# Two transformer blocks on one core: the moving operand of the products read in pairs of tokens 1 KB apart

## The reference, cut to what matters

```
x = first_block(...)     # diff attention + latent attention, then a feed-forward
    h    = rmsnorm(x) * (1 + scale) + shift          # shift, scale, gate from silu(c) @ w_ada + b_ada
    proj = h @ w_in                                  # 3904 columns
    mix  = concat(o_diff, o_mla) @ w_out;  x = x + gate * mix
    f    = square(relu(h2 @ w_ff1)) @ w_ff2          # 2048 -> 8192 -> 2048
    x    = x + gate_f * f;  return rmsnorm(x)
x = second_block(...)    # block-sparse and top-k attention, gated, then a feed-forward
    proj = h @ w_in_2
    y = (sigmoid(ga) * (o_a @ w_moba_out) + sigmoid(gb) * (o_b @ w_dsa_out)) @ w_o
    f = square(relu(h2 @ w_ff1_2)) @ w_ff2_2         # 2048 -> 8192 -> 2048
```

## Time and profile before

| | |
|---|---|
| median of 3 runs | 2734.39 us (2734.12 to 2735.15) |
| profiled execution: span, and its own time as the page gives it | 2736.3 us |
| TensorE matmuls busy | 2649.9 us, 97% |
| VectorE busy | 1938.3 us, 71% |
| ScalarE busy | 1112.3 us, 41% |
| DMA | 658.80 MB, mean 241 GB/s |
| chain that ended last | TensorE 85%, VectorE 7%, DMA 4%, ScalarE 2% |

### The profile page before, as it was taken

One profiled execution on the slowest core, in us unless ns is written; L12 is line 12 of the kernel. 1 busy time (PEld: TensorE's weight loads), 2 busy tenths in 40 slices (PEclk: granted clock), 3 DMA queues, 4 the chain that ended last, 5 costly groups with the idle time before them and its releaser, 6 DMA issues.

```text
span 2736.3 us, 54234 instructions
## 1 busy us (share of the span) xinstructions
PE 2649.9 (97%) x21636; PEld 2485.7 (91%) x21636; DVE 1938.3 (71%) x2030; ACT 1112.3 (41%) x1271; POOL 172.1 (6%) x281
## 2 busy tenths in 40 slices
PE   5999999999999999999998999999999999999998
PEld 2776778899999999998998989999979999999997
DVE  2475586877787776878867888888776565574664
ACT  2333443443343433434333444444444334443443
POOL 5000000101010010110000000001010000000000
PEclk8999999999999999999999999999999999999998
DMA  9997856588888887886766765568847676676763
GB/s 363 368 347 267 264 184 206 190 282 298 284 293 287 274 304 233 294 275 202 252 206 197 223 212 174 163 219 281 285 154 234 196 231 214 193 245 199 231 195 112
DMA packets 304452, 658.80 MB, mean 241 GB/s; under 512 B 31200, under 2 KB 37688, under 8 KB 303928
## 3 DMA queue, kind: packets, MB, share of 16 engines
q1 hardware_dynamic: 272056, 539.35, 58.6%
q0 software_dynamic: 32256, 117.45, 13.3%
HBM read 654.62 MB, written 2.10 MB: 240 GB/s over the span
## 4 chain that ended last, share of the span: by engine, by line
PE 85%; DVE 7%; DMA 4%; ACT 2%; issue 1%; SPq 1%; ACTq 0%; DVEq 0%; POOLq 0%
PE ps L1853 25%; PE ps L1855 24%; PE ps L1854 24%; DVE lo L1039 2%; PE ps L1896 2%; DMA proj<-in_w_ada 2%; PE ps L1898 2%; DMA raw<-in_w_in 2%; PE ps L1897 2%; ACT hi L634 1%; PE ps L2047 1%; DMA ada_ring<-in_w_ada 1%; DVE proj L1211 1%; DVE work L1051 1%; PE ps L1839 1%
## 5 line engine op out<-in xcount | busy, mean ns | idle before, releaser
L1039 DVE TENSOR_TENSOR lo<-raw,hi 128x1024 fp32r<-128x1024 f32 x868 | 1049.5, 1222 | 628.8 <-ACT hi L634 626.9
L634 ACT ACTIVATE hi<-raw 128x1024 fp32r<-128x1024 f32 x868 | 910.4, 1059 | 1267.6 <-PE ps L1855 970.4
L1853 PE MATMUL ps<-acts,hi 128*128 128x256 f32 x4432 | 1247.4, 281 | 21.2 <-DVE lo L1039 13.6
L1854 PE MATMUL ps<-acts,hi 128*128 128x256 f32 x4432 | 1234.3, 279 | 0.0
L1855 PE MATMUL ps<-acts,lo 128*128 128x256 f32 x4432 | 1233.9, 278 | 0.0
L1853 PEld LDWEIGHTS ps<-acts,hi 128*128 128x128 f32 x4432 | 838.7, 189 | 57.5 <-issue 29.9
L1854 PEld LDWEIGHTS ps<-acts,hi 128*128 128x128 f32 x4432 | 836.8, 189 | 1.7 <-issue 1.0
L1855 PEld LDWEIGHTS ps<-acts,lo 128*128 128x128 f32 x4432 | 837.4, 189 | 0.4
L1853 PE MATMUL ps<-f_acts,hi 128*128 128x256 f32 x2048 | 567.6, 277 | 1.4 <-DVE lo L1039 1.3
L1854 PE MATMUL ps<-f_acts,hi 128*128 128x256 f32 x2048 | 565.8, 276 | 0.0
L1855 PE MATMUL ps<-f_acts,lo 128*128 128x256 f32 x2048 | 565.8, 276 | 0.0
(11 more groups left out here) (267 smaller groups left out, 1370.5 us busy)
## 6 DMA issues: line engine op xcount, KB each, us to landing
raw<-in_w_ff SPq DMA_DIRECT2D x512, 512.0 KB, 4.7
raw<-in_w_in SPq DMA_DIRECT2D x232, 512.0 KB, 4.6
ada_ring<-in_w_ada POOLq DMA_DIRECT2D x224, 512.0 KB, 5.0
proj<-in_w_ada SPq DMA_DIRECT2D x92, 512.0 KB, 8.6
ada_ring<-in_w_ada SPq DMA_DIRECT2D x40, 512.0 KB, 6.3
raw<-in_w_out SPq DMA_DIRECT2D x32, 512.0 KB, 5.3
raw<-in_w_o SPq DMA_DIRECT2D x32, 512.0 KB, 5.4
work<-in_w_ada SPq DMA_DIRECT2D x28, 512.0 KB, 6.2
```

The lines of the kernel that those rows point to most:

```text
L634: nc.scalar.activation(hi[n % SPLIT][:, :], raw[n % RAW][:, :], ACT.Copy).then_inc(hi_ready, 1)
L1039: V.tensor_tensor(lo[n % SPLIT][:, :], raw[n % RAW][:, :], hi[n % SPLIT][:, :].bitcast(F32), ALU.subtract)\
L1853: M(out, h, right[:, 0:S], start=start, stop=False)
L1854: M(out, h, right[:, S:2 * S], start=False, stop=False)
```

## The change

Two things change together.

1. The columns of one tile of `acts` and `f_acts` are stored as four runs of 128: high parts of tokens 0 to 127, low parts of tokens 0 to 127, high parts of tokens 128 to 255, low parts of tokens 128 to 255. High parts of token n and token n + 128 are then 256 columns, 1 KB, apart.
2. A product's moving operand still has 256 columns, but in the order n = 0 of both halves, n = 1 of both halves, and so on. PSUM therefore holds token n at column 2n and token n + 128 at column 2n + 1. Each eviction reads every other column (`natural`) and writes two runs of 128 (`halves`), so that all tiles outside `acts` and `f_acts` are as before.

```diff
+        halves = lambda x: x.rearrange("p (a n) -> p a n", a=2) if len(x.shape) == 2 else x.rearrange("p k (a n) -> p k a n", a=2)
+        natural = lambda x: x.rearrange("p (n a) -> p a n", a=2) if len(x.shape) == 2 else x.rearrange("p k (n a) -> p k a n", a=2)
+        places = lambda x: [x.rearrange("p k (a w n) -> p w k a n", a=2, w=2)[:, w] for w in range(2)]
+        acts_hi, acts_lo = places(acts[:, :, :])
+        f_hi, f_lo = places(f_acts[:, :, :])
+        moved = lambda x: x.rearrange("p a n -> p n a")
...
             def product(h, l, right, out, start, stop):
 
-                M(out, h, right[:, 0:S], start=start, stop=False)
-                M(out, h, right[:, S:2 * S], start=False, stop=False)
-                return M(out, l, right[:, 0:S], start=False, stop=stop)
+                right_hi, right_lo = moved(right[0]), moved(right[1])
+                M(out, h, right_hi, start=start, stop=False)
+                M(out, h, right_lo, start=False, stop=False)
+                return M(out, l, right_hi, start=False, stop=stop)
...
-                    xh, xl = acts[:, k, t * P:(t + 1) * P], acts[:, k, S + t * P:S + (t + 1) * P]
+                    xh, xl = acts_hi[:, k, t, :], acts_lo[:, k, t, :]
...
             def plain(dst):
                 def run(left):
-                    V.tensor_copy(dst, left).then_inc(group_out, 1)
+                    V.tensor_copy(halves(dst), natural(left)).then_inc(group_out, 1)
...
-                        last = V.scalar_tensor_tensor(xT[:, tile, :], left[:, j, :], mod(gate, tile), xT[:, tile, :], ALU.mult, ALU.add)
+                        last = V.scalar_tensor_tensor(halves(xT[:, tile, :]), natural(left[:, j, :]), mod(gate, tile), halves(xT[:, tile, :]), ALU.mult, ALU.add)
...
-                    V.tensor_scalar(cross[:, :, :], left, 0.0, None, ALU.max).then_inc(relued, 1)
+                    V.tensor_scalar(halves(cross[:, :, :]), natural(left), 0.0, None, ALU.max).then_inc(relued, 1)
                     dve.wait_ge(relued, k + 1 + dk)
-                    V.tensor_tensor(cross[:, :, :], cross[:, :, :], left, ALU.mult).then_inc(squared, 1)
+                    V.tensor_tensor(halves(cross[:, :, :]), halves(cross[:, :, :]), natural(left), ALU.mult).then_inc(squared, 1)
                     dve.wait_ge(ff_hi, k + 1 + dk)
-                    V.tensor_tensor(f_acts[:, tile, S:2 * S], cross[:, :, :], f_acts[:, tile, 0:S].bitcast(F32), ALU.subtract)\
+                    V.tensor_tensor(f_lo[:, tile], halves(cross[:, :, :]), f_hi[:, tile].bitcast(F32), ALU.subtract)\
                         .then_inc(group_out, 1)
...
-                    V.tensor_tensor(y[:, tile, :], y[:, tile, :], left, ALU.add).then_inc(group_out, 1)
+                    V.tensor_tensor(halves(y[:, tile, :]), halves(y[:, tile, :]), natural(left), ALU.add).then_inc(group_out, 1)
...
-                            last = nc.scalar.activation(acts[:, tile0 + t, 0:S], norm_tmp[:, t, :], ACT.Identity,
+                            last = nc.scalar.activation(acts_hi[:, tile0 + t], halves(norm_tmp[:, t, :]), ACT.Identity,
```

More of the change, by code:

```diff
@@ L645, in group @@
                     act.wait_ge(squared, up + 1 + dup)
-                    nc.scalar.activation(f_acts[:, tile, 0:S], cross[:, :, :], ACT.Copy).then_inc(ff_hi, 1)
+                    nc.scalar.activation(f_hi[:, tile], halves(cross[:, :, :]), ACT.Copy).then_inc(ff_hi, 1)
                 if kind == "gate":
@@ L759, in block_hi @@
                     k = 8 * b + t
-                    last = nc.scalar.activation(acts[:, k, 0:S], block_tmp[:, t, :], ACT.Identity, bias=mods[:, k:k + 1])
+                    last = nc.scalar.activation(acts_hi[:, k], halves(block_tmp[:, t, :]), ACT.Identity, bias=mods[:, k:k + 1])
                 last.then_inc(n_hi, 1)
@@ L1133, in run @@
                 def run(left):
-                    V.tensor_tensor(proj[:, tile, :], proj[:, tile, :], left, ALU.mult).then_inc(group_out, 1)
+                    V.tensor_tensor(halves(proj[:, tile, :]), halves(proj[:, tile, :]), natural(left), ALU.mult).then_inc(group_out, 1)
                 return run
@@ L1140, in run @@
                     dve.wait_ge(group_out, first["dsa"][1] + k)
-                    V.tensor_tensor(cross[:, :, :], proj[:, other, :], left, ALU.mult).then_inc(gated, 1)
+                    V.tensor_tensor(halves(cross[:, :, :]), halves(proj[:, other, :]), natural(left), ALU.mult).then_inc(gated, 1)
                     dve.wait_ge(gated, k + 1)
@@ L1204, in low @@
                     for t in range(a, b):
-                        last = V.scalar_tensor_tensor(acts[:, t, S:2 * S], norm_tmp[:, t, :], shift(t),
-                                                      acts[:, t, 0:S].bitcast(F32), ALU.add, ALU.subtract)
+                        last = V.scalar_tensor_tensor(acts_lo[:, t], halves(norm_tmp[:, t, :]), shift(t),
+                                                      acts_hi[:, t].bitcast(F32), ALU.add, ALU.subtract)
                     last.then_inc(acts_ready, 1)
@@ L1312, in block_low @@
                     k = 8 * b + t
-                    last = V.scalar_tensor_tensor(acts[:, k, S:2 * S], block_tmp[:, t, :], mod(0, k),
-                                                  acts[:, k, 0:S].bitcast(F32), ALU.add, ALU.subtract)
+                    last = V.scalar_tensor_tensor(acts_lo[:, k], halves(block_tmp[:, t, :]), mod(0, k),
+                                                  acts_hi[:, k].bitcast(F32), ALU.add, ALU.subtract)
                 last.then_inc(acts_ready, 1)
@@ L1440, in head_low @@
                     dve.wait_ge(dn_hi, h + 1)
-                    last = V.tensor_tensor(acts[:, 4 * h:4 * h + 4, S:2 * S], work[:, 4 + h, :].rearrange("p (j n) -> p j n", n=S),
-                                           acts[:, 4 * h:4 * h + 4, 0:S].bitcast(F32), ALU.subtract)
+                    last = V.tensor_tensor(acts_lo[:, 4 * h:4 * h + 4], halves(work[:, 4 + h, :].rearrange("p (j n) -> p j n", n=S)),
+                                           acts_hi[:, 4 * h:4 * h + 4].bitcast(F32), ALU.subtract)
                 last.then_inc(o_split, 1)
@@ L1876, in group @@
                             js = slice(j * P, min((j + 1) * P, width))
-                            last = product(h[:, t, js], l[:, t, js], src[:, tile0 + k, :], out[0:js.stop - js.start, at, :],
+                            last = product(h[:, t, js], l[:, t, js], (src[0][:, tile0 + k], src[1][:, tile0 + k]), out[0:js.stop - js.start, at, :],
                                            k == 0 and at % 2 == 0, k == CK * per - 1 and (at % 2 == 1 or at + 1 not in places))
@@ L2025, in start_chunk @@
                         js = slice(j * P, (j + 1) * P)
-                        last = product(h[:, t, js], l[:, t, js], acts[:, k, :], ps[:, 2 * g + j // 2, (j % 2) * S:(j % 2 + 1) * S],
+                        last = product(h[:, t, js], l[:, t, js], (acts_hi[:, k], acts_lo[:, k]), ps[:, 2 * g + j // 2, (j % 2) * S:(j % 2 + 1) * S],
                                        k == 0 and j % 2 == 0, k == KT - 1 and j % 2 == 1)
@@ L2197, in _ @@
                     for t in range(2):
-                        product(h[:, t, j, 0, :], l[:, t, j, 0, :], acts[:, 12 + t, :], out[:, j, :], t == 0, t == 1)
+                        product(h[:, t, j, 0, :], l[:, t, j, 0, :], (acts_hi[:, 12 + t], acts_lo[:, 12 + t]), out[:, j, :], t == 0, t == 1)
                 for q in range(QT):
@@ L2291, in _ @@
                         js = slice(j * P, (j + 1) * P)
-                        last = product(h[:, t, js], l[:, t, js], acts[:, k, :], out[:, j, :], p == out1_first[g] and t == 0 and j % 2 == 0,
+                        last = product(h[:, t, js], l[:, t, js], (acts_hi[:, k], acts_lo[:, k]), out[:, j, :], p == out1_first[g] and t == 0 and j % 2 == 0,
                                        p == out1_last[g] and t == CK - 1 and j % 2 == 1)
@@ L2393, in feed_forward @@
                 for q in range(4):
-                    group(n0 + (4 + q) * FULL, g0 + 4 + q, src=f_acts, fresh={KT - 4: (group_out, g0 + 4)} if q == 0 else None, after=after(q))
+                    group(n0 + (4 + q) * FULL, g0 + 4 + q, src=(f_hi, f_lo), fresh={KT - 4: (group_out, g0 + 4)} if q == 0 else None, after=after(q))
             feed_forward("ff1", "ffn", lambda q: {4: lambda: piece_stats("final", q - 1)} if q else {})
```

46 lines of the change are left out of this document (23 added, 23 removed).

## The result

| | before | after |
|---|---|---|
| median | 2734.26 us (2727.11 to 2735.15, 4 runs) | 2698.41 us (2698.25 to 2702.76, 4 runs) |
| ratio | | 0.9876, 95% interval 0.9851 to 0.9900 |
| profiled span | 2736.3 us | 2696.9 us |

The change makes the kernel 36 us faster. The forecast was 2652, which is 82 us: the direction was right, the size less than half of it. The time still lies just inside the forecast's own range, 2628 to 2700.

The account below looks back on a forecast made before the run. TensorE's matmuls, busy 97% of the span, were taken as the bound: 2736.3 - 85 (94.8 gained less 9.5) + 3 (evictions, copies) = 2654, with the median 1.9 lower, 2652 us; own range 2628 to 2700, with rivals (a) and (c) 2628 to 2816.

Parts of the forecast that it names:

- TensorE is the bound and its spacing is the price: Whole kernel: TensorE's matmuls are busy 97% of the span; a product costs its spacing in the stream, 113.2 or 118.0 ns.
- The loss in line order lies in how the moving operand is read: Products of 256 columns: 6.5 ns of 113.2 are lost by how reads fall, which the new order alters.
- half reading rate: Ground for the gain: two places in turn are each read at half rate, where fp32 passes lose only 2 to 3 ns.
- The two levels come from two streams colliding, the weight load among them: Product streams: an interruption shifts two streams against each other, and the spacing stays at 113.2 or 118.0 ns.
- I take 109.0: Spacing in ns of a product after the change, leaving only the issue loss; gain 24.6 + 70.2 = 94.8 us.
- rival (a): Products: the loss sits in the array or with the weight loads, not in reading order; 2737 us, chance 0.14.
- Slow level in 2,728 matmuls: Ten stretches of TensorE, 322.0 us, stand at 118.0 ns; bringing them to 109.0 gains 24.6 us.
- Give-back of a tenth, 9.5 us: Waits for DMA, such as feed-forward weights, take back a tenth of the 94.8 us gain; 85 us remain.
- Evictions 2 us, copies 1 us, value products 0: Costs: stepped PSUM reads 2 us, split writes of high and low parts 1 us, value groups' untouched moving weights 0.
- Rival (b): All products: each column costs its own fetch, at the fp32 passes' two cycles a column; 4725 us, chance 0.18.
- Rival (c): All products: the new order falls into the slower level, 118.0 ns, everywhere; +80 us, 2814 us, chance 0.09.

Follow-up runs that it names:

- e6: The kernel before, in line order, with 32 of 128 weight columns in 14 of 16 feature tiles: 2730.24 us.
- e1: A kernel of only 60-matmul fp32r streams, varying reading order, distance and weights: 256 columns in line 113.5 or 117.8 ns, pairs 111.7 ns.
- e4: A kernel of only matmul streams, varying weight widths, shifts, closer pairs, 512 columns and bf16: pairs 111.7 ns with 128 weight columns, 109.2 with 96.
- e8: A kernel of only matmul streams with other numbers of moving and weight columns: 111.7 ns beside 128 weight columns for 128 to 256 moving columns in pairs.
- e5: The changed kernel, in pairs, with 32 of 128 weight columns in 14 of 16 feature tiles: 2661.91 us.
- e2: The changed kernel with its four runs of 128 kept, but products and evictions reading in line: 2734.02 us, ratio 0.9997 to the kernel before.
- e9: The changed kernel run once more, unaltered, for a comparison on one chip: 2699.84 us, ratio 0.9881 to the kernel before.
- e10: The changed kernel with the value groups' moving weights also read in pairs: 2693.13 us, ratio 0.9861 to the kernel before.

## Why the prediction was off, step by step

- **TensorE is the bound and its spacing is the price: right.** The span followed TensorE's busy time, 39.4 of 45.9 us.
- **The loss in line order lies in how the moving operand is read: right.** e6 and the narrow and equal-column streams of e1 leave it at 113.7, bf16 doesn't have it (109.2), and alternating two places takes it away. The prediction's half reading rate as a ground is not borne out, though: four places in turn read each at a quarter rate, and stand at 142. That the alternation works is shown; why is open.
- **The two levels come from two streams colliding, the weight load among them: not borne out.** The slow level went with the change (three stretches above), as expected, but e4 has both levels beside 16 weight columns, and no other engine is at work in those streams. Weights do bear on line order (64 columns 119.0, shifts 117.3 to 120.0 in e1), but no run ties the levels to them. What sets the level after an interruption stays open.
- **"I take 109.0" for a product with 128 weight columns: the failed step.** The floor of 109.0 was worked out from rows at two cycles a moving column, where a weight load of 128 columns has 213 ns or more to hide in. No row of before had fp32r weights beside a moving operand that could have gone faster than they, and the weight load was costed at nothing. It takes 111.7 ns (e8) and now sets the pace; e5, where it is narrow, has the forecast's pace and most of the missing time. Redone with 111.7, the term is 2,728 x (118.0 - 111.7) = 17.2 and 16,712 x (113.2 - 111.7) = 25.1, 42.3 us where 94.8 stood. The forecast itself named "the weight loads, which are as before" only in rival (a), as the place of the whole loss, and not as a second limit just under the first. The upper end of its own range, 2700, was for a stream that sheds less than the whole loss, without a word on what would stop it; that the time fell inside is luck, as far as the cause goes.
- **Slow level in 2,728 matmuls: a little low.** By the distances of starts some 3,560 gaps were at 117.8; that lifts 42.3 toward the 45.9 measured. In e2, in the same order, it was some 1,990: this share differs from run to run.
- **Give-back of a tenth, 9.5 us: about right in size.** 6.5 us went to TensorE's waits. The rows show where: TensorE's largest wait, before and after (5.7 us more), then ScalarE's after (90.9 before).

```profile
PE ps L1853 <- DVE lo L1039: 14.9, 8, 5.3
...
PE ps L1861 <- DVE lo L1046: 20.6, 13, 4.9
...
ACT hi L641 <- DMA raw<-in_w_ff: 125.9, 63, 3.9
```

  The first 205 us, at a DMA share of 0.95, gave nothing: they hold 1,249 matmuls now (1,258 in e9), 1,258 before.
- **Evictions 2 us, copies 1 us, value products 0:** 0 for all three, by the rows above. "Whichever way the reads go" missed that the value groups had the same loss to shed, 576 x 13 ns (e10).
- **Rival (a), the loss is not in the order of reading:** it would have shown 1,502 matmuls in 170 us and 2737 us. 1,524 and 2698 stand there, so it fell; but what it said of the weight loads holds for the last 2.5 ns.
- **Rival (b), a fetch for every column:** not for pairs, at any distance from 16 bytes to 8 KB. But its price, two cycles a column (216.3), is about what eight places (220 to 247 ns) and a step of two or four columns (230, 233) pay. The Trainium skill's page "SBUF — State Buffer", section "Door 1: The DMA port swizzle", asks for two hits in a 16-byte line; pairs 1 KB apart, with one hit at a time, run at full rate, while a step of two columns, with two hits in a line, halves it. The measurement decides: for this operand the rule holds in neither case, though a step of four columns, with one hit in a line, does pay (233). The Trainium skill's page "TensorE: Matmul & The Clock Gate", section "Back-to-back issue gap", gives N / 2.4 + 2.5 ns as the gap of a matmul by itself. Here it fits streams: bf16 (109.2) and pairs beside up to 124 weight columns (109.2), or with 512 moving columns (215.8). fp32r in line stands above it, and 256 moving columns beside 128 weight columns do too (111.7).
- **Rival (c)** would have shown 1,440 matmuls in 170 us; 1,524 stand there.

## What to carry to other kernels

When a loss is taken out of one of two things that run side by side, price the other one by itself first: the gain ends at the second limit, here 2.5 ns short of the pace of the moving reads (111.7 against 109.2). For a tight stream of matmuls count them in an undisturbed window, since the mean of one hardly moves. And kernels of nothing but short streams, some twenty kinds in a run of 450 to 610 us, told what the large kernel could not: that pairs may stand as close as 16 bytes, that four places are worse than one, and where the rest had gone.

## What the runs showed of the hardware, unexpected

- An fp32r moving operand read in line costs 113.3 to 113.5 or 117.8 ns for 256 columns at 2.4 GHz, and 227 to 231 for 512 (e4, e8). Read from two places in turn, 1 KB apart, it costs 109.2 and 215.8; bf16 in line costs 109.2 too.
- At distances from 16 bytes to 8 KB pairs cost 111.7 beside 128 weight columns. That is the pace of the weight load, so a difference of up to 2.5 ns between distances would not have shown.
- Four places in turn cost 142 to 143 ns, eight 220 to 247, a step of two columns 230 (e1).
- An fp32r weight load takes two cycles a column and 5.0 ns (111.7 ns for 128, 58.3 for 64, e8). With 128 weight columns it limits any matmul whose moving operand is read in pairs and has fewer than some 262 columns ((111.7 - 2.5) x 2.4, an estimate). In bf16, 128 moving columns beside 128 weight columns stand at 55.8 ns (e8), so that weight load takes no longer.
- VectorE and ScalarE read every other column of PSUM at full pace: for 1,024 elements 1216 ns on VectorE (1217 in line), and 1007 ns on ScalarE for the exponential of the gates (1010 in line).
